# Feed-forward gate and up products with the weight tile stationary and the activation rows moved

## The reference

```python
h = rms_norm(x, norm_ffn[l])
x = x + (jax.nn.silu(h @ w_gate[l]) * (h @ w_up[l])) @ w_down[l]
```

## Time and profile before

| what | value |
|---|---|
| median of 3 runs | 1428.78 us (1428.46 to 1428.87) |
| span of the profiled execution, first to last instruction | 1427.1 us |
| TensorE products: busy, number | 1417.4 us, 7738 |
| TensorE weight loads: busy, number | 1181.2 us, 7738 |
| VectorE busy | 927.8 us |
| ScalarE busy | 803.7 us |
| GpSimd busy | 80.8 us |
| mean DMA rate | 172 GB/s |

### The profile page before, as it was taken

How to read it: one execution, slowest core, us unless ns; L and a number is a source line. 1 busy time by engine, 2 the same in 40 slices (tenths; PEclk the granted TensorE clock), 3 DMA queues, 4 the chain that set the end, 5 groups by cost and what they waited for, 6 DMA issues and landing times.

```text
span 1427.1 us, 19775 instructions
## 1 busy us (share of the span) xinstructions
PE 1417.4 (99%) x7738; PEld 1181.2 (83%) x7738; DVE 927.8 (65%) x1282; ACT 803.7 (56%) x1297; POOL 80.8 (6%) x86
## 2 busy tenths in 40 slices
PE   9999999999999999999999999999999999999998
PEld 8887888888888878888888888888888888888886
DVE  5698765565567988555556788655555789655554
ACT  6775554444467654544445788544444788544443
POOL 0113100000002220000000000000000000000001
PEclk9999999999999999999999999999999999999999
DMA  8744456655375445476564524566653634556651
GB/s 285 225 150 125 157 165 204 195 188 191 108 226 177 148 137 167 158 219 196 189 183 141 166 91 160 177 208 207 191 180 108 216 104 148 177 193 192 188 188 52
DMA packets 174509, 245.46 MB, mean 172 GB/s; under 512 B 18880, under 2 KB 117840, under 8 KB 174416
## 3 DMA queue, kind: packets, MB, share of 16 engines
q1 hardware_dynamic: 174224, 244.11, 54.4%
q10 hardware_dynamic: 192, 0.08, 0.0%
HBM read 243.10 MB, written 1.05 MB: 171 GB/s over the span
## 4 chain that ended last, share of the span: by engine, by line
PE 96%; DVE 1%; ACT 1%; DMA 0%; issue 0%; POOL 0%; POOLq 0%; SPq 0%; ACTq 0%
PE acc L565 19%; PE acc L568 18%; PE acc L571 18%; PE misc L565 10%; PE misc L568 10%; PE misc L571 10%; PE misc L659 3%; PE misc L925 1%; PE misc L726 1%; PE misc L667 1%; PE misc L701 1%; DVE arena L1873 1%; PE misc L878 1%; PE misc L879 1%; DVE w_lo L1443 0%; PE misc L876 0%
## 5 line engine op out<-in xcount | busy, mean ns | idle before, releaser
L1443 DVE TENSOR_TENSOR w_lo<-w_raw,w_hi 128x1024 fp32r<-128x1024 f32 (+2 forms) x466 | 554.7, 1206 | 269.4 <-ACT w_hi L1028 267.7
L1028 ACT ACTIVATE w_hi<-w_raw 128x1024 fp32r<-128x1024 f32 (+2 forms) x466 | 478.0, 1041 | 276.6 <-PE misc L571 164.0
L565 PE MATMUL acc<-w_hi,h_hi 128*128 128x512 f32 (+2 forms) x768 | 206.7, 390 | 1.0 <-ACT h_hi L1067 0.8
L568 PE MATMUL acc<-w_lo,h_hi 128*128 128x512 f32 (+2 forms) x768 | 198.9, 380 | 0.0
L571 PE MATMUL acc<-w_hi,h_lo 128*128 128x512 f32 (+2 forms) x768 | 198.5, 379 | 0.0
L565 PE MATMUL misc<-w_hi,h_hi 128*128 128x512 f32 x640 | 175.5, 396 | 0.0
L568 PE MATMUL misc<-w_lo,h_hi 128*128 128x512 f32 x640 | 171.5, 390 | 0.0
L571 PE MATMUL misc<-w_hi,h_lo 128*128 128x512 f32 x640 | 171.5, 390 | 0.0
L568 PEld LDWEIGHTS acc<-w_lo,h_hi 128*128 128x128 f32 x768 | 140.7, 188 | 27.9 <-DVE w_lo L1443 0.5
L571 PEld LDWEIGHTS acc<-w_hi,h_lo 128*128 128x128 f32 x768 | 140.9, 188 | 27.0
L565 PEld LDWEIGHTS acc<-w_hi,h_hi 128*128 128x128 f32 x768 | 135.0, 188 | 26.1 <-ACT arena L1103 1.3
(11 more groups left out here) (229 smaller groups left out, 1179.7 us busy)
## 6 DMA issues: line engine op xcount, KB each, us to landing
w_raw<-in_w_in SPq DMA_DIRECT2D x112, 512.0 KB, 4.4
w_raw<-in_w_gate SPq DMA_DIRECT2D x176, 256.0 KB, 2.9
w_raw<-in_w_up SPq DMA_DIRECT2D x176, 256.0 KB, 3.2
w_raw<-in_w_down SPq DMA_DIRECT2D x88, 512.0 KB, 3.7
w_raw<-in_w_out SPq DMA_DIRECT2D x40, 512.0 KB, 4.2
w_raw<-in_w_in SPq DMA_DIRECT2D x16, 336.0 KB, 4.3
w_raw<-in_w_proj_a SPq DMA_DIRECT2D x8, 512.0 KB, 4.1
w_raw<-in_w_proj_b SPq DMA_DIRECT2D x8, 512.0 KB, 4.2
```

What stands on the lines that cost most here:

```text
L565: pe.matmul(dst, st[0][:, k, t * P:(t + 1) * P], rhs, start=first, stop=False)
L568: pe.matmul(dst, st[0][:, k, t * P:(t + 1) * P], rhs, start=False, stop=False)
L1028: act.activation(w_hi[:, g % RING, 0:w], w_raw[:, g % RING, 0:w], ACT.Copy)\
L1443: dve.tensor_tensor(w_lo[:, g % RING, 0:w], w_raw[:, g % RING, 0:w], w_hi[:, g % RING, 0:w].bitcast(F32), ALU.subtract)\
```

## The change

- `h_hi` and `h_lo` become two views of one tensor, next to each other for each k tile; the four `misc` banks become views of one PSUM tensor.
- Gate and up products of steps 1 to 10 (`gate_up_turned`) load a 128 x 128 tile of the weights and move the 256 rows of `h`: eight cells for each slot (two k tiles, four column tiles n of 128), each with three products into columns 0 to 255 of bank misc n: `w_hi` x `h_hi` and `w_hi` x `h_lo` one after the other, and after the wait for `w_lo` all `w_lo` x `h_hi`. That is 24 products for each slot. The result has hidden columns on partitions and rows in columns: gate in misc0 and misc1, up in misc2 and misc3.
- Step 0 stays as it was. Its `f_act` is turned in an idle `acc` bank (`turn_first`); `turn(1)` to `turn(10)` are gone.
- The inverse norm becomes a row `r_row`, once for each layer: two transposes of a broadcast column and a copy. VectorE multiplies the gate by it (`f_gate`, 128 x 512), ScalarE takes silu, VectorE multiplies with up, ScalarE copies to `st_hi`, VectorE makes `st_lo`, both from SBUF. The inverse norm on the up side is applied at the layer's end, in the residual add (`scaled_residual`).
- `st` tiles alternate between 0, 1 and 2, 3 from step to step. The calls of `split_until` in the feed-forward part are placed anew.

```diff
-        h_hi = sb("h_hi", [P, KD, T], F32R)
-        h_lo = sb("h_lo", [P, KD, T], F32R)
+        h_both = sb("h_both", [P, KD, 2, T], F32R)
+        h_hi, h_lo = h_both[:, :, 0, :], h_both[:, :, 1, :]
...
+                def gate_up_turned(g, behind, between=None):
+
+                    pe.wait_ge(*DV_.at(layer, behind))
+                    for q in range(4):
+                        if between is not None and q == 2:
+                            between()
+                        cells = [(misc[n], 2 * q + kk, slice(kk * 512 + n * P, kk * 512 + n * P + P))
+                                 for kk in range(2) for n in range(4)]
+                        r = (g + q) % RING
+                        pe.wait_ge(*AC.of("hi", g + q))
+                        for bank, tile, cols in cells:
+                            pe.matmul(bank[:, 0:T], w_hi[:, r, cols], h_hi[:, tile, :], start=tile == 0, stop=False)
+                            pe.matmul(bank[:, 0:T], w_hi[:, r, cols], h_lo[:, tile, :], start=False, stop=False)
+                        pe.wait_ge(*DV_.of("lo", g + q))
+                        for bank, tile, cols in cells:
+                            mm = pe.matmul(bank[:, 0:T], w_lo[:, r, cols], h_hi[:, tile, :], start=False,
+                                           stop=tile == KD - 1)
+                        mm.then_inc(*PE.slot("used", g + q))
+
+                def turn_first():
+
+                    spare = acc[2 * o.pair["wo1"]:2 * o.pair["wo1"] + 2]
+                    pe.wait_ge(*DV_.at(layer, "wo1.t1"))
+                    pe.wait_ge(*PO.at(layer, "r.mT"))
+                    for t in range(NT):
+                        c = RS + M_Y + t
+                        tr = pe.transpose(spare[1][:, t * P:(t + 1) * P], bc(small[:, c:c + 1], [P, P]), ident)
+                    tr.then_inc(*PE.mark("r_row"))
+                    pe.wait_ge(*DV_.at(layer, "f0"))
...
-                down(g + 8, 0)
-                turn(1)
                 g += 10
-                for i in range(2, FSTEPS - 1):
-                    gate_up(g, i, behind=f"f{i - 1}")
+                for i in range(2, FSTEPS):
+                    gate_up_turned(g, f"f{i - 1}")
                     down(g + 4, i - 1)
-                    turn(i)
                     g += 6
-                gate_up(g, FSTEPS - 1, behind=f"f{FSTEPS - 2}")
-                down(g + 4, FSTEPS - 2, between=FSTEPS - 1)
...
+                def silu_turned(s, i):
+                    split_until(layer, s + 4 + LOOK)
+                    if i < FSTEPS - 1:
+                        split_until(layer, s + 5 + LOOK)
+                    act.wait_ge(*DV_.at(layer, f"gate{i}"))
+                    act.activation(f_silu, f_gate, ACT.Silu).then_inc(*AC.mark(f"f{i}"))
+                    act.wait_ge(*DV_.at(layer, f"f{i}"))
+                    at = 2 * (i % 2)
+                    act.activation(st_hi[:, at:at + 2, :], f_act, ACT.Copy).then_inc(*AC.mark(f"fT{i}"))
...
-                def turned(s_end, i):
-                    split_until(layer, s_end + LOOK)
...
+                def gated_turned(s, i):
+                    split_until(layer, s + 4 + LOOK)
+                    dve.wait_ge(*PE.of("used", BASE[layer] + s + 3))
+                    dve.wait_ge(*DV_.now(layer))
+                    dve.tensor_tensor(f_gate, misc_all[:, 0:2, 0:T], bc(r_row.rearrange("p (a t) -> p a t", a=1), [P, 2, T]),
+                                      ALU.mult).then_inc(*DV_.mark(f"gate{i}"))
+                    if i < FSTEPS - 1:
+                        split_until(layer, s + 5 + LOOK)
+                    dve.wait_ge(*AC.at(layer, f"f{i}"))
+                    dve.tensor_tensor(f_act, misc_all[:, 2:4, 0:T], f_silu, ALU.mult).then_inc(*DV_.mark(f"f{i}"))
                     dve.wait_ge(*AC.at(layer, f"fT{i}"))
...
+                    at = 2 * (i % 2)
+                    hi, lo = (v[:, at:at + 2, :] for v in stat["st"])
+                    dve.tensor_tensor(lo, f_act, hi.bitcast(F32), ALU.subtract).then_inc(*DV_.mark(f"fT{i}"))
```

More of the change, by code:

```diff
@@ L890, in feed_forward, with gate_up @@
                 base = BASE[layer] + o.ffn0
-                def gate_up(g, i, behind, between=None):
-                    pe.wait_ge(*DV_.at(layer, behind))
-                    banks = acc[2 * o.pair["wo0"]:2 * o.pair["wo0"] + 2] if i == 0 else misc[2:4]
+                def gate_up(g):
+                    pe.wait_ge(*DV_.at(layer, "wo0.t1"))
+                    banks = acc[2 * o.pair["wo0"]:2 * o.pair["wo0"] + 2]
                     for q in range(4):
-                        if between is not None and q == 2:
-                            turn(between)
-                        if i == 0 and q == 1:
+                        if q == 1:
                             shared(layer, "mT2")
@@ L949, in down_sweep, with down @@
                     return mm
-                def down(g, i, between=None):
+                def down(g, i):
                     for q in range(2):
-                        if between is not None and q == 1:
-                            turn(between)
                         down_sweep(g + q, i, down_cells(g + q, i, range(2)), q == 0).then_inc(*PE.slot("used", g + q))
@@ L1547, in residual, with scaled_residual @@
                     dve.tensor_tensor(v, v, b[:, :], ALU.add).then_inc(*DV_.mark(name))
+            def scaled_residual(layer, banks, names):
+                for (half, t, b), name in zip(banks, names):
+                    v = x[:, t, half * 512:half * 512 + 512]
+                    c = RS + M_Y + t
+                    dve.scalar_tensor_tensor(out=v, in0=b[:, :], scalar=small[:, c:c + 1], in1=v, op0=ALU.mult,
+                                             op1=ALU.add).then_inc(*DV_.mark(name))
             n = [3]
@@ L1605, in feed_forward, with gated_first @@
                 o = ORD[layer[0]]
-                def gated(s_end, i):
-                    split_until(layer, s_end + LOOK)
+                def gated_first(s):
+                    split_until(layer, s + 3 + LOOK)
                     for t in range(NT):
-                        dve.wait_ge(*AC.at(layer, f"f{i}.t{t}"))
-                        b = acc[2 * o.pair["wo0"] + t] if i == 0 else misc[2 + t]
-                        c = RS + M_Y + t
-                        dve.scalar_tensor_tensor(out=f_act[:, t, :], in0=b[:, FW:2 * FW], scalar=small[:, c:c + 1],
-                                                 in1=f_silu[:, t, :], op0=ALU.mult, op1=ALU.mult)\
-                            .then_inc(*DV_.mark(f"f{i}"))
@@ new lines, in gated_first @@
+                    dve.wait_ge(*AC.at(layer, "fT0"))
+                    hi, lo = (v[:, 0:2, :].rearrange("p k t -> p (k t)") for v in stat["st"])
+                    dve.tensor_tensor(lo, acc[2 * o.pair["wo1"]][:, :], hi.bitcast(F32), ALU.subtract)\
+                        .then_inc(*DV_.mark("fT0"))
+                def gated_turned(s, i):
+                    split_until(layer, s + 4 + LOOK)
+                    dve.wait_ge(*PE.of("used", BASE[layer] + s + 3))
[6 more added lines that the diff above has]
+                    dve.tensor_tensor(f_act, misc_all[:, 2:4, 0:T], f_silu, ALU.mult).then_inc(*DV_.mark(f"f{i}"))
@@ L1658, in feed_forward @@
                 dve.wait_ge(*PE.of("used", BASE[layer] + o.slots - 1))
-                residual(layer, [(1, 1, acc[3])], ["x_ffn3"])
+                scaled_residual(layer, [(1, 1, acc[3])], ["x_ffn3"])
                 if layer != LAYERS[-1]:
```

102 lines of the change are left out of this document (47 added, 55 removed).

## The result

The changed kernel takes **1437.03 us** (median of 4 runs, 1436.58 to 1437.59) against 1428.77 us (1428.46 to 1428.87) of the kernel before: ratio 1.0059 [1.0044, 1.0073], slower by 8.3 us. Forecast were 1430.9 us, that is +2.1, and a range of 1424 to 1440. The time lies in the range, four times as far from the kernel before as the forecast, and next to the rival "the fixed cost stays whole", which had 1437.4 us. The profiled executions have spans of 1434.8 and 1427.1 us, so the trace has 7.7 us of the difference to show, at a granted clock of 1.00 in the step compared.

The account below looks back on a forecast made before the run. The prediction took TensorE's queue of products as the bound. Gate and up products +19.0, transposes removed -19.6, row of norms +1.0 and seams +1.7 summed to +2.1 us, 1430.9 us, range 1424 to 1440.

Parts of the forecast that it names:

- the fixed cost stays whole: Rival for gate and up products: 13.3 ns fixed, 120 ns a product, +25.5 instead of +19.0, 1437.4 us; chance 25 in 100.
- What bounds the kernel: Whole kernel: a queue of products on TensorE, 96% of the chain, priced by starts rather than busy time.
- The gate and up products: Steps 1 to 10 of four layers: 48 products of 512 columns become 96 of 256 at 118.3 ns, +19.0 us.
- The range and the number: Whole kernel: 1430.9 us, range 1424 to 1440, taking in 117 and 120 ns a product with 2 us more for seams and transposes.
- starts at 120 ns or more: Sign in the changed trace's gate-up slots that would make the prediction wrong; it expected starts 118.3 ns apart.
- Loads stay hidden: Gate and up products: a weight load's 112 ns stays below the product's 118, some 6 ns of room, so no cost.
- Equal weights, one bank: Gate-up pairs: adding into one bank region costs nothing; rival, second product without fixed cost, 14.8 us saved, 1416.1 us, chance 10.
- The transposes: Activation transposes of steps 1 to 10: 40 groups of four go, 0.49 us of queue each, -19.6 us.
- The row of inverse norms: Once per layer: two transposes of 0.12 us turn the norm into a row, 8 in all, +1.0 us.
- The chain at a step's end: Last gate-up product to f(i): about 3.4 us, covered by 5.44 us of down products; 2 us left, no wait.
- The seams: Between layers: two VectorE splits ahead of the first norm operand delay TensorE by +0.5, +0.6 and +0.6, +1.7 us.
- Sum: Whole kernel: 19.0 - 19.6 + 1.0 + 1.7 = +2.1 us, span 1429.2, time 1430.9 us.

Follow-up runs that it names:

- cut kernel: The kernel before with gate and up products of steps 1 to 10 cut into two of 256 columns, transposes kept: 1452.13 us, ratio 1.0165.
- bare kernel: Everything but long runs of TensorE products left out, each length in its own run: 119.8 ns between starts at 256 columns, 125.3 or 126.7 at 272.
- Mended alone: The changed kernel with the splits of the next layer's slots 1 and 2 back in the last step: 1435.91 us, ratio 1.0051.

## Why the prediction was right or wrong

**What bounds the kernel**: right. TensorE is 96% of the chain before and after, and pricing by starts accounts for the step: 96 x 120.0 + 24 x 226.7 ns = 16.96 us of 16.98.

**The gate and up products**: this is the term that was mis-sized. The step that failed is "the nearest long, undisturbed row, 272 columns at 125.0 ns, less 16 columns" = 118.3 ns. Measured are 120.0 in each of 40 steps: +25.6 us instead of +19.0. The row was long and undisturbed, but it doesn't lie on the line of the others; the 512 and 384-column rows, with 13.4 and 13.3 ns of fixed cost, did, and both gave 120. One row off the line was trusted above two on it because it was nearer, as if the fixed cost fell with the length. The 256-column row after an idle stretch, 120 ns, was right; the busy one, 117, was three products behind others, and the first products behind another length do start 117 or 118 ns apart in the cut kernel too. Where the 13.3 ns come from no run shows.

**The range and the number**: by its own sign, starts at 120 ns or more, the forecast failed, and the rival that it gave 25 in 100 against its own 40 took place. The time lies in the range because the range was made to take in this rival. That the rival's 1437.4 us come within 0.4 of the measured time is in part luck: its row of norms and its seams were together 0.6 us too dear, the changes of length, 0.8, were missing, and the start of the run differs by about 1 us from one execution to the next.

**Loads stay hidden**: right, at 120.0 ns a product. The 112 for a load is less sure than it looked: the row of 64 columns that was read as eight products is four f32 products, each shown twice with a load each, as in the bare kernel. The rule of the Trainium skill (TensorE: Matmul & The Clock Gate, the section on packing small matmuls), by which loads overlap products only where row groups differ (it also names a background weight buffer that a load can go to ahead of its product), was given nothing, rightly: 1920 added full-array loads cost 25.6 us, not over 200. The Trainium skill's N/2.4 + 2.5 ns for the gap between products (same page, the section on the back-to-back issue gap), which it gives for an isolated product and not for a stream of loads and products, is 109 ns at 256 columns and does not agree with 120.0 here.

**Equal weights, one bank**: no gain and no loss. Same weights or new, 120.0; in bare runs one weight tile or one bank, 119.9.

**The transposes**: right, -19.6 forecast, -20.1 alone (by the steps of that kernel's trace, 40 x 0.493 = 19.7). 1.9 of it are the slow starts of the nine products behind each group.

**The row of inverse norms**: +1.0 was too much. Its eight transposes start 0.11 us apart, 0.9 us. Per layer the feed-forward part is 1.82 us longer, ten steps of 0.167 make 1.67, and 0.15 is left for the row: 0.6 in all, since the group of step 0 now stands in front of 256-column products and costs 0.06 us less a layer.

**A change of length**: missing from the sum. The change brings products of 256 columns next to those of 512. The first ones behind the change start 234, 236, 229, 232 and 231 ns apart, and the way back gives 7 ns back: +0.02 us a step, +0.8 in all.

**The chain at a step's end**: right that it doesn't wait. It takes 3.18 us (1315.38 to 1318.56) where 3.4 was forecast, and 2.3 us of cover are left.

**The seams**: right in place, number and size: +0.45, +0.55 and +0.55 by starts, 1.55 against 1.7. Mended alone they gave back 1.5 at the seams and 1.1 in the time.

**Sum**: the 7.7 us of the spans are 6.7 of the steps (40 x 0.167: 25.6 - 19.7 + 0.8), 0.6 of the rows, 1.5 of the seams, and -1.1 at the start of the run, ahead of the first feed-forward part: the first gate-up product of step 1 starts at 213.1 us before and 212.1 after, and at 212.2 to 213.1 in the nine other kernels, none of which changes TensorE's work ahead of it. The forecast had +2.1. What it lacked, 5.6, is 6.6 of the one term and 0.8 of the changes of length, less 0.4, 0.1 and 0.1 of the rows, the seams and the transposes, and the 1.1 of the start.

## What to carry to other kernels

Price a new product length from the line through all lengths that the trace shows, not from the nearest row alone, and keep a row that is off the line as a bound. Where a term is multiplied by thousands (here 3.84 us for each ns), the forecast is as good as that number, and three-product rows don't give it. A layout that saves a transposition can double the products; if two of them share their weights, move both operands in one product and add the halves afterwards, where the other engines have cover: here that, with the seams mended, made +8.3 us into -7.5, and with two slots at a time into -9.1.

## What was not expected of the hardware

- The pace of a load and its product depends on the first words of its moved rows and of its weights in bare runs: 113.3 to 122.7 ns at 256 columns, 226.7 to 233.3 at 512. It was not reproduced exactly from run to run, and a shift of 16 words did nothing in the kernel.
- The first five products of 512 columns behind ones of 256 start 229 to 236 ns apart instead of 227, and the first nine behind f32 transposes 224 to 236. With the lengths alternating the price was 6 ns a pair, less than the 20 ns at the border of two longer runs.
- A wait of TensorE shown as 1.30 us cost 1.57 us: it is counted from the shown end of the last product, 0.16 us after the next could have started, and the product behind the first one follows it by 0.22 instead of 0.12 us.
